# A mixer layer's depthwise convolution as 64x64 fp32 products on 16 phases, and another order of the front's additions, squares and norms

## The reference

```
x  = x + pos_embed_2d
hx = rmsnorm(x, g_pre) * (1 + sc) + sh          # sc, sh from silu(c) @ w_mod
ux = hx @ w_in                                   # 2304 columns = 18 tiles of 128
v_lru, g_lru, v_pool, g_pool, v_conf, gg_conf, g_conf = split(ux)
y_lru  = bidirectional RG-LRU (width-4 conv, sigmoid gates by 64x64 blocks, scans)
y_pool = centred mean pooling (windows 2, 4, 8, 16) minus identity, 64x64 products
z      = v_conf * sigmoid(gg_conf)               # 256 channels
z      = dwconv(z, conf_dw (31 taps), conf_dw_b) # each channel over positions
z      = silu(layernorm(z) * ln_g + ln_b)
y_conf = z @ conf_pw
o      = concat(y_lru*silu(g_lru), y_pool*silu(g_pool), y_conf*silu(g_conf)) @ w_out
out    = x + gt * rmsnorm(o, g_post)
```

## Time and profile before

| | |
|---|---|
| runs | 775.5, 777.88, 778.16 us (median 777.88) |
| profiled execution | 776.39 us, of which the span (first to last instruction) is 774.3 us |
| mean granted PE clock | 0.971 of full speed |
| PE busy | 723.8 us |
| DVE, ACT, POOL busy | 519.9, 463.4, 218.4 us |
| DMA | 130.11 MB, 168 GB/s over the span |

### The profile page before, as it was taken

How to read it: one execution, slowest core, us unless ns; L and a number is a source line. 1 busy time by engine, 2 the same in 40 slices (tenths; PEclk the granted TensorE clock), 3 DMA queues, 4 the chain that set the end, 5 groups by cost and what they waited for, 6 DMA issues and landing times.

```text
span 774.3 us, 10037 instructions
## 1 busy us (share of the span) xinstructions
PE 723.8 (93%) x3548; PEld 566.7 (73%) x3548; DVE 519.9 (67%) x807; ACT 463.4 (60%) x756; POOL 218.4 (28%) x262
## 2 busy tenths in 40 slices
PE   3885989999999999999999989799999999999997
PEld 1573767767777778767877767677787888888885
DVE  4377752776899799687995765577746574756422
ACT  4166653599898996897896972333554142534311
POOL 0022334110431254123431055322211244434321
PEclk9698999999999999999999999989999999999999
DMA  9998002444354555345444045345378767867531
GB/s 362 359 322 264 14 36 74 110 110 126 112 164 124 154 160 180 111 133 164 151 147 140 34 157 167 81 125 166 106 247 283 252 212 255 301 199 252 175 131 60
DMA packets 89219, 130.11 MB, mean 168 GB/s; under 512 B 22769, under 2 KB 54129, under 8 KB 87633
## 3 DMA queue, kind: packets, MB, share of 16 engines
q1 hardware_dynamic: 84800, 115.44, 45.5%
q0 software_dynamic: 4368, 14.03, 6.8%
HBM read 91.17 MB, written 38.27 MB: 167 GB/s over the span
## 4 chain that ended last, share of the span: by engine, by line
PE 74%; ACT 7%; DVE 6%; issue 5%; DMA 5%; POOL 2%; SPq 1%; DVEq 0%; ACTq 0%; POOLq 0%
PE bank L1506 23%; PE bank L1508 22%; PE bank L1507 22%; PE bank L1586 4%; DMA wm<-in_w_mod 3%; DVE xg L1160 1%; ACT bank L861 1%; ACT fbuf L878 1%; POOL xTh L604 1%; DVE xTl L1168 1%; ACT Ib L908 1%; PE bank L1542 1%; DMA pv<-scratch_u 1%; DVE xg L1140 1%; PE bank L1634 1%
## 5 line engine op out<-in xcount | busy, mean ns | idle before, releaser
L1506 PE MATMUL bank<-xTh,wh 128*128 128x512 f32 (+1 forms) x592 | 238.5, 403 | 10.4 <-DVE xTl L1168 4.8
L1508 PE MATMUL bank<-xTh,wl 128*128 128x512 f32 (+1 forms) x592 | 230.8, 390 | 0.0
L1507 PE MATMUL bank<-xTl,wh 128*128 128x512 f32 x576 | 226.5, 393 | 0.0
L1506 PEld LDWEIGHTS bank<-xTh,wh 128*128 128x128 f32 x592 | 112.7, 190 | 45.6 <-issue 13.1
L1508 PEld LDWEIGHTS bank<-xTh,wl 128*128 128x128 f32 x592 | 112.4, 190 | 23.6
L1507 PEld LDWEIGHTS bank<-xTl,wh 128*128 128x128 f32 x576 | 109.7, 190 | 21.7 <-issue 1.2
L1506 PE MATMUL bank<-xTh 128*128 128x512 f32 (+1 forms) x272 | 104.2, 383 | 1.7 <-issue 1.1
L1507 PE MATMUL bank<-xTl,xTh 128*128 128x512 f32 x256 | 99.6, 389 | 0.0
L1508 PE MATMUL bank<-xTh,xTl 128*128 128x512 f32 x256 | 99.6, 389 | 0.0
L894 ACT ACTIVATE ustage<-bank 128x512 f32<-128x512 f32 x56 | 32.5, 591 | 77.8 <-PE bank L1508 77.8
L1506 PEld LDWEIGHTS bank<-xTh 128*128 128x128 f32 x272 | 51.1, 188 | 12.1 <-issue 2.3
(11 more groups left out here) (189 smaller groups left out, 1397.4 us busy)
## 6 DMA issues: line engine op xcount, KB each, us to landing
scratch_u<-ustage SPq DMA_DIRECT2D x72, 256.0 KB, 3.6
wraw<-in_w_in SPq DMA_DIRECT2D x18, 512.0 KB, 4.9
wm<-in_w_mod SPq DMA_DIRECT2D x8, 1024.0 KB, 14.4
xg<-in_x SPq DMA_DIRECT2D x16, 512.0 KB, 9.4
yb<-scratch_y SPq DMA_DIRECT2D x32, 256.0 KB, 3.5
gb<-scratch_u SPq DMA_DIRECT2D x32, 256.0 KB, 5.1
xres<-in_x SPq DMA_DIRECT2D x16, 512.0 KB, 4.7
out<-tout SPq DMA_DIRECT2D x15, 512.0 KB, 3.0
```

The lines of the kernel that those rows point to most:

```text
L1506: mm(out, wh_, xh_, start=first, stop=False)
L1507: mm(out, wh_, xl_, start=False, stop=False)
L1508: return mm(out, wl_, xh_, start=False, stop=last)
```

## The change

The convolution uses 16 phases of 128 positions with 8 channels in 128 rows; so 3 shifts do. One unit (`j`) takes 16 channels as two halves of 128 rows x 2; in each half the upper 64 rows (4 channels) and the lower 64 are separate products of 64x64 in plain fp32, with no high and low parts. Units go in pairs, c and c+1: c uses the quarters upper-upper and lower-lower, c+1 the two crossed ones, so the channels of odd units come out in exchanged halves, and bias, LayerNorm and pointwise parameters are permuted on the host (`conv_order`). Weights and z have 4 slots each. Pairs stand behind every fourth projection from the 22nd. The bias is added in `ln_sum` and `ln_centre`. The tiles that feed the convolution are stored in runs of 32 numbers, and `load_ln` reads runs of 32 numbers with four DMAs in place of two.

In the front, an addition stands one slot ahead of the low part and of its square; the square sums and the norm of the next group stand behind all eight low parts; ACT's slot is one modulation and one square for all groups, and evacuations are moved to the first slot and the end of a group.

```diff
-PHASES = 8
+PHASES = 16
-N_CONV = 256 // GROUP_CH
+N_CONV = 256 // (2 * GROUP_CH)
-CONV_FROM = 20
-Z_SLOTS = 3
+CONV_FROM = 22
+CONV_SLOTS = 4
-        if n >= CONV_FROM and (n - CONV_FROM) % 2 == 0 and convs < N_CONV:
-            units.append(("conv", convs))
-            convs += 1
+        if n >= CONV_FROM and (n - CONV_FROM) % 4 == 0 and convs < N_CONV:
+            units += [("conv", convs), ("conv", convs + 1)]
+            convs += 2
...
-    return [g for g in range(N_CONV) if GATES_AFTER[q] <= CONV_AT[g] - lead - (g > 0) < STEP_END[q]]
+    return [g for g in range(N_CONV) if GATES_AFTER[q] <= CONV_AT[g - g % 2] - lead - (g > 1) < STEP_END[q]]
...
-                    src = cv_dram[8 * i:8 * i + 8].rearrange("g (c j) n -> (g c) j n", j=PHASES)
-                    g.dma_start(phases(la[:, i, :], CH // PHASES), src[:, :, part]).then_inc(s_la, 16)
+                    src = cv_dram[N_CONV * i:N_CONV * i + N_CONV].rearrange("g (c j) n -> (g c) j n", j=PHASES)
+                    dst = phases(la[:, i, :], CH // PHASES)
+                    for js in (slice(0, PHASES // 2), slice(PHASES // 2, PHASES)):
+                        g.dma_start(dst[:, js], src[:, js, part]).then_inc(s_la, 16)
...
+            for gi in range(1, NCH):
+                for k in range(KD):
+                    modulate(gi, [k])
+                    if k == 0:
+                        evac(3 if gi == 1 else N_CU + 2 * gi - 4)
+                    squares(gi + 1, 1 - k // TPC, [k % TPC])
+                root(gi + 1)
+                if gi > 1:
+                    evac(N_CU + 2 * gi - 3)
+            modulate(NCH, [0])
+            evac(N_CU + 2 * NCH - 4)
+            modulate(NCH, range(1, KD))
+            evac(N_CU + 2 * NCH - 3)
...
+            def add(gi, k):
+                (add_cols if k < TPC else add_rows)(gi, [k % TPC])
+            for gi in range(1, NCH):
+                add(gi + 1, 0)
+                for k in range(KD):
+                    if k + 1 < KD:
+                        add(gi + 1, k + 1)
+                    lo_group(gi, [k])
+                square_sums(gi + 1)
+                normalise(gi + 1)
...
+            def conv_pair(n, c):
+                top, low = slice(0, 64), slice(64, 128)
+                for j in (c, c + 1):
+                    pe.wait_ge(s_cwr[j % CONV_SLOTS], 16 * (j // CONV_SLOTS + 1))
+                pe.wait_ge(s_cz, c + 2)
+                pe.wait_ge(s_ev, evacuations_before(N_CU + n + 1))
+                for h in range(2):
+                    for m in range(SHIFTS):
+                        for j in (c, c + 1):
+                            to = (top, low) if j == c else (low, top)
+                            for x, o in zip((top, low), to):
+                                ins = mm(pu[N_CU + n + j - c][o, h * NPH:(h + 1) * NPH], cw[x, j % CONV_SLOTS, h, m, :],
+                                         cz[x, j % CONV_SLOTS, h, m:m + NPH], start=m == 0, stop=m == SHIFTS - 1)
+                            if h == 1 and m == SHIFTS - 1:
+                                ins.then_inc(s_pu, 1)
...
-                v.tensor_tensor(out=lq[:, 0, :], in0=la[:, 0, :], in1=la[:, 1, :], op=ALU.add).then_inc(s_las, 1)
+                    link(v.tensor_tensor(out=bsum, in0=par_col("conf_dw_b", 0), in1=par_col("conf_dw_b", 1), op=ALU.add))
+                stt(lq[:, 0, :], la[:, 0, :], bsum, la[:, 1, :], ALU.add, ALU.add).then_inc(s_las, 1)
```

More of the change, by code:

```diff
@@ L173, in mixer_kernel @@
         MID_BYTES = a3.off - r0 - 4 * (CTX + SEQ)
[L174 to L180, removed]
+        cw = a3.take("cvw", [P, CONV_SLOTS, 2, SHIFTS, P // 2])
+        cg = a3.take("cvg", [P, CONV_SLOTS, 2, NPH])
+        cz = a3.take("cvz", [P, CONV_SLOTS, 2, NPH + 2 * REACH])
         wgp = a3.take("wgp", [P, KD, P])
@@ L284, in mixer_kernel @@
         s_czero, s_cgs, s_cz = sem("conf_zeroed"), sem("conf_sigmoid"), sem("conf_glu")
-        s_czh, s_czl = sem("conf_z_hi"), sem("conf_z_lo")
-        s_cl = [sem(f"conf_in{b}") for b in range(Z_SLOTS)]
-        s_cwr, s_cwhi, s_cwlo = [sem(f"convw_in{b}") for b in range(2)], sem("convw_hi"), sem("convw_lo")
+        s_cl = [sem(f"conf_in{b}") for b in range(CONV_SLOTS)]
+        s_cwr = [sem(f"convw_in{b}") for b in range(CONV_SLOTS)]
         s_dve = sem("dve_chain")
@@ L483, in load_conv_w @@
             def load_conv_w(j):
-                if j >= 2:
-                    sp.wait_ge(s_pu, N_CU + CONV_AT[j - 2] + 1)
-                sp.dma_start(cwraw[:, j % 2], conv_dw[j]).then_inc(s_cwr[j % 2], 16)
+                if j >= CONV_SLOTS:
+                    sp.wait_ge(s_pu, N_CU + CONV_AT[j - CONV_SLOTS] + 1)
+                sp.dma_start(cw[:, j % CONV_SLOTS], conv_dw[j]).then_inc(s_cwr[j % CONV_SLOTS], 16)
             def load_conv_z(j):
-                if j < Z_SLOTS:
-                    sp.wait_ge(s_czero, 2)
-                else:
-                    sp.wait_ge(s_pu, N_CU + CONV_AT[j - Z_SLOTS] + 1)
-                half, rows_ = divmod(j, P // GROUP_CH)
-                for tile, dst in ((V_CONF + half, cz), (GG_CONF + half, cg)):
+                b = j % CONV_SLOTS
+                if j < CONV_SLOTS:
+                    sp.wait_ge(s_czero, 1)
+                else:
+                    sp.wait_ge(s_pu, N_CU + CONV_AT[j - CONV_SLOTS] + 1)
+                half, first = divmod(2 * GROUP_CH * j, P)
+                for tile, dst in ((V_CONF + half, cz[:, b, :, REACH:REACH + NPH]), (GG_CONF + half, cg[:, b])):
                     for c in range(NCH):
@@ L679, in weights_hi @@
                     done_w += 1
[L680 to L688, removed]
             W2 = CH + 2 * PH
@@ L888, in evac @@
                 elif o == "conv":
-                    ins = a.activation(ustage[:, U % U_SLOTS, 0:NPH], pu[U][:, 0:NPH], ACT.Identity,
-                                       bias=par_col("conf_dw_b", c))
+                    ins = a.activation(ustage[:, U % U_SLOTS, 0:2 * NPH], pu[U][:, 0:2 * NPH], ACT.Copy)
                 elif ORDER[o] in CONV_TILES:
@@ L1325, in weights_lo @@
                     done_w += 1
-                while done_cw < N_CONV and CONV_AT[done_cw] - 4 <= upto:
-                    conv_w_lo(done_cw)
-                    done_cw += 1
             conv(0)
@@ L1719, in banded @@
     import numpy as np
-    out = np.zeros((N_CONV, GROUP_CH, PHASES, SHIFTS, GROUP_CH, PHASES), w.dtype)
-    grouped = w.reshape(CONF_K, N_CONV, GROUP_CH)
+    half = GROUP_CH // 2
+    out = np.zeros((N_CONV, GROUP_CH, PHASES, 2, SHIFTS, half, PHASES), w.dtype)
+    grouped = w.reshape(CONF_K, N_CONV, 2, GROUP_CH)
     for m in range(SHIFTS):
@@ L1727, in banded, with conv_order @@
                     for c in range(GROUP_CH):
-                        out[:, c, j, m, c, i] = grouped[k, :, c]
-    return out.reshape(N_CONV, P, SHIFTS, P)
+                        out[:, c, j, :, m, c % half, i] = grouped[k, :, :, c]
+    return out.reshape(N_CONV, P, 2, SHIFTS, P // 2)
+def conv_order(v):
+    rows = v.reshape((N_CONV, 2, 2, GROUP_CH // 2) + v.shape[1:]).copy()
+    rows[1::2] = rows[1::2, :, ::-1]
+    return rows.reshape(v.shape)
 def kernel(**inputs):
```

116 lines of the change are left out of this document (24 added, 92 removed).

## The result

The changed kernel takes 792.75 us (median of 4 runs, 791.53 to 795.25), the kernel before 777.86 (775.5 to 778.16): a ratio of 1.0209, 95% interval [1.0175, 1.0243]. It is slower by some 15 us, where the forecast was 763.

A forecast was written before the change was run, and what follows sets the result against it. PE, busy 93% of the span, was taken as the bound. Front -10, convolution -14.5, middle +2.5 and tail +7.5 summed to -14.5 us, giving 763 us from 777.9, range 753 to 773.

The forecast's parts named there:

- Part 1: Convolution on PE: 28.2 us of products removed, eight pairs at 1.66 us (13.3) added; gain taken as 14.5 us.
- Rival A: Convolution on PE: quarters miss the column rate, sets 0.22 us apart, gain falls by 10.4, time 773; chance 0.1.
- Part 2: Middle, gates 0 to 19: ACT falls behind in uneven steps and gives back 2.5 us, between 0 and +8.
- rival C: Middle: ACT sets the pace, so all of the convolution's gain is given back, about 774 us; chance 0.1.
- upper end of +8: Middle: the most ACT was expected to give back, about half the convolution's gain, in us.
- Part 3: Front, to about 135 us: additions one slot ahead and later norms save 10 us, bounds 7 to 12.
- ACT is the bound at 1.34: Front: with additions one slot ahead, ACT's slot of one modulation and one square takes 1.34 us and sets the pace.
- lower bound of 7: Front: smallest gain expected, in us, with a low clock at each chunk or rows landing late.
- Part 4: Tail, LayerNorm: four cv load DMAs in place of two lengthen the chain by 7.5 us, between 2 and 12.
- rival B: Tail: the cv load stays hidden, so the tail adds only 1 to 2 us, time 757; chance 0.14.
- Rival D: cv loads and convolution tile stores: 128-byte runs slow them beyond their number, kernel slower at 787 us; chance 0.06.

The follow-up runs named there:

- less work for ACT: Changed kernel with cv loads on SP and four staging slots, plus ACT's two square roots per gate step cut to one column (wrong coefficients): 746.51 us.

## Why the prediction was wrong, point by point

The forecast's sum was -14.5, the profiled executions differ by +17.1 in span: 31.6 us off. The front missed by 3.0, the middle by 14.0, the tail by 14.6; 4.1 us of the tail's loss are the middle's mechanism, ACT late behind gates 19, so by cause it is 18.1 for part 2 and 10.5 for part 4.

**Part 1, the convolution on PE: right.** 1.66 us a pair were forecast and measured, 24 products in place of 30 of twice the columns. Rival A is out. The estimate from the Trainium skill ("TensorE: Matmul & The Clock Gate", Wait — 56ns, not 53.3ns?), 62 ns for each product where the sequencer decodes in software, made a pair 0.2 us longer. The trace doesn't show it: the pair kept to 1.66. Nothing on PE kept the 14.5 us from arriving.

**Part 2, what the middle gives back: this step failed in mechanism and size, 16.5 us (304.6 - 302.6 + 14.5) and 4.1 behind gates 19, in place of 2.5.** The step asked whether ACT's work fits in PE's step, on average and in the long steps. It didn't ask what stands between ACT and the next bank. ACT, once late, has four banks to empty in a row; a pair adds two of them at once, and the fourth copy needs a slot whose store has not landed. The trace of before has no such wait to read. The fourth slot gave 7.8 us of interval back (304.4 to 296.6), and less work for ACT the remaining 8.6. So rival C, ACT paces the middle, was the right mechanism for half of it; its chance of 0.1 was too low with ACT at 88% busy. Of the step's own argument, that ACT falls behind in uneven steps, the version with pairs from the 20th shows 2.8 us. The upper end of +8 was passed by ACT's share alone (8.6).

**Part 3, the front: mechanism right, size 7.0 in place of 10.** The second transposition came at 71.54, as forecast (71). The next two came 18.4 and 17.5 us apart, not 16.0. The term that failed is "ACT is the bound at 1.34". DVE after, in chunk 2's second half:

```profile
81.29 1.12 DVE L1135 TENSOR_TENSOR xTl<-fbuf,xTh 128x512 fp32r<-128x512 f32 x1
82.33 0.68 DVE L1113 TENSOR_TENSOR xg<-xg,posr 128x512 f32<-128x512 f32 x1
82.93 1.10 DVE L1135 TENSOR_TENSOR xTl<-fbuf,xTh 128x512 fp32r<-128x512 f32 x1
83.95 0.68 DVE L1113 TENSOR_TENSOR xg<-xg,posr 128x512 f32<-128x512 f32 x1
```

Here a slot of DVE is 1.64 us (81.29 to 82.93) with no idle time, since a low part takes 1.10 where it took 0.69 in the first slots, and ACT waits for it: its last four slots (78.55 to 85.40) take 6.85 us where 5.4 were forecast, +1.5. The square sums and the norm then stand behind DVE's last low parts: the norm starts 1.5 us behind ACT's last square where 0.9 were forecast, +0.6, and the transposition 3.0 us behind that start, not 2.75. That makes the 2.4 us. Why a low part takes longer there isn't shown. The lower bound of 7 was just met.

**Part 4, the tail: this step failed in "POOL spends 1.85 us on issuing two (475.41), so 3.7 on four".** Four took 7.6: 2.74 + 3.99 + 0.88. Three issues fit the descriptor memory, the fourth didn't, so doubling a measured 1.85 passed a limit that the rows of before never touched. The wait's 13.0 us were missing: three places in the chain at 4.0, and 1.0 more; PE is also 3.4 us busier behind gates 19 than without the wait (320.6 and 317.3), at a granted clock of 0.96 and 0.98. Without the wait the tail is 338.4, 9.1 over before. That lies inside the 5.5 to 9.5 forecast by luck, as 4.1 of it is lost to ACT ahead of the first mean product, and only 5.0 are left for the load. This is near the 5.5 of issue alone: DVE's sums don't wait for the load at all, and what counts is POOL's issue ahead of `lsh`, where the 7.5 taken leaned on the landing. With the four issues off POOL 7.5 of the 9.1 go too (330.9). I had named the order on POOL's queue as the reason against rival B, and then sized it by the transfer.

**Rival D** gave 787 and the right sign, by the wrong mechanism: the load's DMAs land 3.9 us behind their issue at the median, where the longer ones of before took 4.9, and not 2.5 times that. The Trainium skill's rule that spoke for it ("DMA: Bandwidth & Descriptors", Specifications, on runs under 512 bytes) is borne out in part: 128-byte stores land later than the same stores wide (4.3 and 2.7 us at the median), but the time doesn't change with them, and the loads show no such price. The forecast's reading that 256-byte stores cost nothing compared stores at different places; the same 16 stores took 3.6 us at the median with 256-byte runs. What the short runs of the load cost is descriptors. The range's lower and upper ends came from bounds around each term as costed; none of them allowed for a full memory or for slots, which are limits that no row of before showed.

## What to carry to other kernels

Where a change multiplies a resource in use (descriptors of a DMA, banks that come full together), work out how many fit before pricing the step by proportion: a limit that was never reached leaves no row in the trace of before. An engine that is 88% busy beside the bound, as ACT was here, can be late in bursts once the bound gets faster, so ask for the length of the burst and compare it with the slots behind it, not only its mean with the step. Keep DMAs of many short runs off an engine whose next instruction somebody waits for; here moving the four loads of cv to SP's queue was worth 20.5 us, more than the change's whole gain on PE.

## What the runs showed of the hardware

- A DMA of 1024 runs issued by POOL takes 0.9 us of POOL, and one of 128 runs 0.55. SP takes 0.37 to 0.58 us on each of the first three of a load, and 0.64 to 2.54 on the fourth.
- With 4096 bytes of descriptor memory three DMAs of 1024 runs are issued without a wait, with 4352 four, with 2048 one.
- The next one then stands until the DMA issued last before it has landed, and starts 0.30 to 0.43 us later, in all 20 cases of three kernels. The wait is 2.3 to 4.6 us long, as that landing comes. The first DMA's landing doesn't end it: for chunk 2 of the kernel after it comes at 505.54 us, and the fourth issue starts at 508.14.
- Twelve sets of four records of 64x64 fp32 products with 128 columns and the change of mode around them take 1.66 us, and the sets start 0.109 us apart.
- The 16 stores in 128-byte runs land 4.3 us behind their issue at the median, the same stores in 2 KB runs 2.7. The time shows no difference (792.75 and 792.77 us).
